# Two heads' masks first, then both heads' score products, in stick breaking and in FoX

## The reference, cut to what matters

```python
# stick breaking, 16 heads of width 64, scale 64**-0.5
z = jnp.einsum('bhtd,bhsd->bhts', qb, kb) * scale
strict = s_idx < t_idx
log_1m = jnp.where(strict, jax.nn.log_sigmoid(-z), 0.0)
suffix = lax.cumsum(log_1m, axis=3, reverse=True) - log_1m
a = jnp.where(strict, jnp.exp(jax.nn.log_sigmoid(z) + suffix), 0.0)
outs.append(jnp.einsum('bhts,bhsd->bhtd', a, vb))

# FoX, 8 heads of width 64, Fc = cumulative sum of the forget gates' logarithms
s = jnp.einsum('bhqd,bhkd->bhqk', qh, kh) * scale + Fc[..., :, None] - Fc[..., None, :]
p = jax.nn.softmax(jnp.where(mask, s, -jnp.inf), axis=-1)
outs.append(jnp.einsum('bhqk,bhkd->bhqd', p, vh))
```

## Time and profile before

| what | value |
|---|---|
| median of 3 runs | 1332.75 us (1332.71 to 1333.68) |
| the profiled execution's own time | 1331.95 us |
| its span, first to last instruction | 1330.2 us |
| DVE busy | 854.0 us (64%) |
| ACT busy | 708.3 us (53%) |
| DMA, mean rate | 168 GB/s |

### The profile page before, as it was taken

The page is one execution under the profiler, slowest core; times in us unless marked ns, Lnnn a source line. Parts: engine busy times, 40 slices in busy tenths (PEclk is TensorE's granted clock), DMA queues, the critical chain, the costliest instruction groups (busy, mean ns, idle before and its releaser), DMA issues.

```text
span 1330.2 us, 17683 instructions
## 1 busy us (share of the span) xinstructions
PE 1307.8 (98%) x7329; PEld 1124.8 (85%) x7329; DVE 854.0 (64%) x995; ACT 708.3 (53%) x968; POOL 110.7 (8%) x177
## 2 busy tenths in 40 slices
PE   7999999999999999999999999999999999999999
PEld 6888898988888988879888888898867888788887
DVE  4556755766666644367576666667875666787775
ACT  5655544544444676765454444565555764655553
POOL 7200100100000100020100000101330003000000
PEclk9999999999999999999999999999999999899999
DMA  8744643555555543244255555553434345455552
GB/s 257 254 159 142 210 149 118 183 190 188 191 189 207 167 158 127 96 159 159 95 190 191 190 190 191 181 197 96 159 127 158 129 156 176 140 190 190 190 191 95
DMA packets 156113, 223.64 MB, mean 168 GB/s; under 512 B 6103, under 2 KB 107635, under 8 KB 156032
## 3 DMA queue, kind: packets, MB, share of 16 engines
q1 hardware_dynamic: 154240, 218.18, 49.7%
q0 software_dynamic: 1664, 4.27, 1.0%
q10 hardware_dynamic: 128, 0.05, 0.0%
HBM read 221.44 MB, written 1.05 MB: 167 GB/s over the span
## 4 chain that ended last, share of the span: by engine, by line
PE 92%; DVE 4%; ACT 2%; POOL 1%; issue 1%; DMA 1%; SPq 0%; POOLq 0%; ACTq 0%
PE ps L397 18%; PE ps L399 9%; PE ps L421 9%; PE ps L423 9%; PE ps L422 9%; PE ps L382 5%; PE ps L383 5%; PE ps L384 5%; PE ps L559 4%; PE ps L560 4%; PE ps L561 4%; DVE wlo L1563 1%; PE ps L850 1%; PE ps L446 1%; ACT whi L1061 1%; PE ps L494 1%
## 5 line engine op out<-in xcount | busy, mean ns | idle before, releaser
L1061 ACT ACTIVATE whi<-raw 128x1024 fp32r<-128x1024 f32 x412 | 426.1, 1052 | 363.6 <-PE ps L397 167.4
L1563 DVE TENSOR_TENSOR wlo<-raw,whi 128x1024 fp32r<-128x1024 f32 x411 | 493.4, 1230 | 196.1 <-ACT whi L1061 192.8
L397 PE MATMUL ps<-RR,whi 128*128 128x512 f32 x1056 | 366.1, 397 | 0.8 <-DVE RR L1593 0.8
L399 PE MATMUL ps<-RR,wlo 128*128 128x256 f32 x1056 | 273.9, 280 | 0.1
L421 PE MATMUL ps<-whi,RR 128*128 128x512 f32 x592 | 237.5, 401 | 3.7 <-DVE ar L1626 1.6
L423 PE MATMUL ps<-whi,RR 128*128 128x512 f32 x592 | 231.0, 390 | 0.0
L422 PE MATMUL ps<-wlo,RR 128*128 128x512 f32 x592 | 230.9, 390 | 0.0
L397 PEld LDWEIGHTS ps<-RR,whi 128*128 128x128 f32 x1056 | 191.3, 188 | 37.8 <-DVE wlo L1563 1.2
L399 PEld LDWEIGHTS ps<-RR,wlo 128*128 128x128 f32 x1056 | 199.9, 189 | 12.3 <-DVE RR L1593 0.4
L382 PE MATMUL ps<-RR,whi 128*128 128x256 f32 x512 | 147.0, 287 | 1.7 <-DVE RR L1593 1.3
L383 PE MATMUL ps<-RR,whi 128*128 128x256 f32 x512 | 144.9, 283 | 0.0
(11 more groups left out here) (333 smaller groups left out, 1288.7 us busy)
## 6 DMA issues: line engine op xcount, KB each, us to landing
raw<-in_ffn_w_gate_up SPq DMA_DIRECT2D x44, 1024.0 KB, 5.1
raw<-in_ffn_w_down SPq DMA_DIRECT2D x33, 1024.0 KB, 4.9
raw<-in_w_in SPq DMA_DIRECT2D x28, 1024.0 KB, 5.0
raw<-in_ffn_w_up SPq DMA_DIRECT2D x22, 1024.0 KB, 5.1
raw<-in_xa_w_kv SPq DMA_DIRECT2D x16, 1024.0 KB, 5.2
raw<-in_sb_w_qkv SPq DMA_DIRECT2D x12, 1024.0 KB, 5.1
raw<-in_ml_w_in SPq DMA_DIRECT2D x11, 1024.0 KB, 5.7
raw<-in_xa_w_q SPq DMA_DIRECT2D x8, 1024.0 KB, 5.2
```

The source lines that it names most:

```text
L397: m = pe.matmul(two(ps[:, bank, :]), p.hi[:, k, :], XT2[:, k, :, :], start=k == 0, stop=k == 7)
L399: pe.matmul(ps[:, bank, 0:256], p.lo[:, k, :], X.h[:, k, :], start=False, stop=False)
L1061: act.activation(p.hi, p.raw, ACT.Copy).then_inc(S["w_hi"], 1)
L1563: dve.tensor_tensor(p.lo, p.raw, p.hi.bitcast(F32), ALU.subtract).then_inc(S["w_lo"], 2 if p.n == 2 else 1)
```

## The change

`sb_scores(p)` now issues the masks of both heads, then line 708's product of both heads, then line 709's product of both heads. `sb_z` is raised three times a pair (by the second head's first product and by both heads' last) and ACT waits for all three. `fox_head` becomes `fox_pair(g, j)`, with masks and selector products of both heads first and the f32 products of both heads behind them; `fx_s` is raised six times a group. PE's order around FoX is changed: `mqb` tile 1 now comes ahead of the wait for `fqT` and `fkT`; the pairs stand after `mqb` tile 1 and `gate0a` tile 1, and after `gate2a` tile 1 and `gate2b` tile 1. The wait for `yb_lo` moves behind `gate2a` tile 1.

```diff
             def sb_scores(p):
-                for h in range(2):
-                    o = ps[:, 4 + 2 * (p % 2) + h, :]
-                    r = slice(64 * h, 64 * h + 64)
+                both = [(ps[:, 4 + 2 * (p % 2) + h, :], slice(64 * h, 64 * h + 64)) for h in range(2)]
+                for o, r in both:
                     pe.matmul(o[:, 0:128], identb[:, :], mStr[:, :], start=True, stop=False, skip_group_check=True)
                     pe.matmul(o[:, 256:384], identb[:, :], mStr[:, :], start=False, stop=False, skip_group_check=True)
-                    pe.matmul(o[:, 0:256], kT[r, p, 0:128], qT[r, p, :], start=False, stop=False, skip_group_check=True)
+                for o, r in both:
+                    m = pe.matmul(o[:, 0:256], kT[r, p, 0:128], qT[r, p, :], start=False, stop=False, skip_group_check=True)
+                m.then_inc(S["sb_z"], 1)
+                for o, r in both:
                     m = pe.matmul(o[:, 256:384], kT[r, p, 128:256], qT[r, p, 128:256], start=False, stop=False,
                                   skip_group_check=True)
-                m.then_inc(S["sb_z"], 1)
+                    m.then_inc(S["sb_z"], 1)
...
-            def fox_head(g, h4):
...
+            def fox_pair(g, j):
+                n = 2 * g + j
+                both = [(ps[:, 4 + 2 * j + i, :], slice(64 * i, 64 * i + 64)) for i in range(2)]
+                for i, (o, r) in enumerate(both):
+                    sel = selr[:, 2 * n + i:2 * n + i + 1].to_broadcast([128, 128])
+                    pe.matmul(o[:, 0:128], identb[:, :], mRow[:, :], start=True, stop=False, skip_group_check=True)
+                    pe.matmul(o[:, 256:384], identb[:, :], mRow[:, :], start=False, stop=False, skip_group_check=True)
+                    pe.matmul(o[:, 0:128], sel, lg[:, 0:128], start=False, stop=False, skip_group_check=True)
+                    pe.matmul(o[:, 128:384], sel, lg, start=False, stop=False, skip_group_check=True)
+                for o, r in both:
+                    m = pe.matmul(o[:, 0:128], fqT[r, n, 0:128], fkT[r, n, 0:128], start=False, stop=False, skip_group_check=True)
+                m.then_inc(S["fx_s"], 1)
+                for o, r in both:
+                    m = pe.matmul(o[:, 128:384], fqT[r, n, 128:256], fkT[r, n, :], start=False, stop=True, skip_group_check=True)
                     m.then_inc(S["fx_s"], 1)
...
             tm_tile("mqb", X, 4, 8, 0, 0)
+            tm_tile("mqb", X, 4, 8, 1, 1)
...
-            fox_head(0, 0)
-            tm_tile("mqb", X, 4, 8, 1, 1)
-            fox_head(0, 1)
+            fox_pair(0, 0)
             pe.wait_ge(*at("fv_act", 1))
             tm_tile("gate0a", X, 0, 8, 2, 0)
-            fox_head(0, 2)
             pe.wait_ge(*at("f_cc", 1))
             tm_tile("gate0a", X, 0, 8, 3, 1)
-            fox_head(0, 3)
+            fox_pair(0, 1)
...
             tm_tile("gate2a", X, 0, 8, 2, 0)
-            pe.wait_ge(S["yb_lo"], 1)
-            fox_head(1, 0)
             pe.wait_ge(S["gate"], 2)
             tm_tile("gate2a", X, 0, 8, 3, 1)
-            fox_head(1, 1)
+            pe.wait_ge(S["yb_lo"], 1)
+            fox_pair(1, 0)
             tm_tile("gate2b", X, 4, 8, 2, 0)
-            fox_head(1, 2)
             tm_tile("gate2b", X, 4, 8, 3, 1)
-            fox_head(1, 3)
+            fox_pair(1, 1)
...
-                    act.wait_ge(S["sb_z"], i + 1)
+                    act.wait_ge(S["sb_z"], 3 * i + 3)
...
-                dve.wait_ge(S["fx_s"], g + 1)
+                dve.wait_ge(S["fx_s"], 6 * g + 6)
```

## The result

The changed kernel takes 1318.81 us (median of 4 runs, 1318.04 to 1319.46), the kernel before 1332.91 us in the same comparison (4 runs): a ratio of 0.9894, 95% interval 0.9881 to 0.9906. That is 14.1 us less; 1319.7 had been forecast. The two profiled executions took 1331.95 and 1319.46 us, 12.5 apart.

A forecast was written before the change was run, and what follows sets the result against it. PE was taken to bound the kernel; stick breaking's 7.1 and FoX's 5.9 us sum to 13.0, from 1331.95 to 1318.9, and with the median 0.8 above, 1319.7 us. Range 1317.5 to 1324.0.

The forecast's parts named there:

- What bounds the kernel: Whole kernel: PE, busy 98% of the span with 92% of the last chain, so shortening PE's order shortens the kernel.
- Side by side by row halves: Score parts: two heads on different row halves overlap wholly, so a pair costs one head's 0.85 us.
- first rival: Score parts: passes start strictly in issue order, overlap is partial, 2.6 us lost, 1322.3; chance 0.17 shared with loads in turn.
- Stick breaking: Eight pairs save 0.93 us each, 7.4 us, less 0.3 for a new wait: 7.1 us.
- new wait at the third pair: Stick breaking's third pair: PE waits 0.2 to 0.3 us for ACT's line 1344, and only there.
- FoX: Four pairs save 1.09 us each, 4.4 us, plus 1.5 for the covered wait: 5.9 us.
- covered wait: Ahead of FoX's first head: `mqb` tile 1 moved forward covers PE's idle of 1.52 us, saving 1.5 us.
- the entry: FoX: going from line 920's full-array product to the first f32 product costs 0.14 us, saved once a pair.
- the return: FoX: the projection behind the scores takes 0.10 us more to come back, saved once a pair.
- The sum: Whole kernel: stick breaking 7.1 plus FoX 5.9 saves 13.0 us.
- No case for slower: Slower rival, score parts: each change of row half stops PE, at 0.24 us making 1336.1 us; chance 0.03.
- The clock: PE's late stall: a fall from 2.4 to 1.2 GHz costs up to 2.4 us; 2 us either way.

The follow-up runs named there:

- products issued by head: Changed kernel with the first head's two products issued before the second head's two, in stick breaking and FoX: 1318.72 us, ratio to before 0.9888.
- the same half twice: Changed kernel with both heads of a pair reading rows 0 to 63, the first head's scores computed twice: 1325.77 us, ratio to before 0.9941.
- the changed kernel again: Changed kernel, unaltered, measured once more against the kernel before on another set's chip: 1319.04 us against 1332.37, ratio 0.9895.

## Why the prediction was right

*What bounds the kernel*: right. PE's order was shortened, and what it lost reached the end within the scatter of the stretches between and behind (0.4 us).

*Side by side by row halves*: right, taken over from the column halves of the earlier trace rows. The score part of a pair is 0.86 us against 0.85 forecast. The second half's passes start 0.007 to 0.014 us after the first half's. The products issued by head and the same half twice show that this is what it is. The first rival, passes strictly in the order of issue, is ruled out for row halves.

*Stick breaking*: 7.1 forecast, 7.43 measured. A pair saves 0.95 in place of 0.93, as the third and fourth masks follow 0.056 apart and not 0.07. The new wait at the third pair is there, 0.14 us and not 0.3. ACT's absolute value starts at 482.17, 0.11 ahead of the end of the copy before it (482.28), and not after it as I had reckoned; its wait of 0.50 us is gone, as forecast. With the 0.40 us taken off by which this trace's stick breaking starts later, that is 481.77 against the 481.93 reckoned: the 0.16 by which the new wait is shorter.

*FoX*: 5.9 forecast, 5.72 measured. The covered wait gave 1.68 and not 1.5, as the run with it alone shows. A pair gave the remaining 4.04 / 4 = 1.01 us and not 1.09. Two terms of that were mis-sized. One is the entry: I took line 920's product to need 0.12 us as one of line 382 does, but the next full-array product follows it after 0.17 (976.46 to 976.63). So to enter costs 0.26 - 0.17 = 0.09, as in stick breaking (0.08), and not 0.14. The other is the return: the first projection product behind a pair has 0.36 us to the second (977.99 to 978.35), and behind a single head 0.33, so a pair doesn't save the whole 0.10.

*The sum*: that 13.0 lies so near 13.15 is partly luck. Stick breaking came out 0.33 over its term, FoX's pairs 0.36 under theirs (4.04 against 4.4) and the covered wait 0.18 over.

*No case for slower*: the price of going from one half to the other is nothing that the traces show, 0.01 us instead of the 0.24 of that rival.

*The clock*: of either sign, as said, but the price was over-sized: 0.5 to 1.3 us, not up to 2.4. I had also cut its length at the end of my window: in the trace of before the half level goes on behind it, 0.77 on average from 1144 to 1148 us. And PE was not mostly idle in that window, as the forecast says, but busy for 4.73 of 7.80 us.

The clock explains a part of why the medians lie 14.1 apart and the stages 13.15. The medians of before were between 1332.37 and 1333.53 from one comparison to the next, those of the changed kernel 1318.81 and 1319.04. Seven of the 22 runs of before for which the clock is on record beside the experiments have a mean granted clock of 0.996, and they take 1333.53 to 1335.71 us; no run of the changed kernel is below 0.997. At 0.999, in the comparison of the changed kernel again, before takes 1331.76 and 1331.83 us and the changed kernel 1318.54 to 1319.09, 12.7 to 13.3 apart, as the stages say. So the gain is about 13 us. That the last 1 us of the 14.1 comes from such runs of the kernel before is likely and not shown: in that comparison its clocks are not on record, and none of the runs at 0.996 was traced. The changed kernel's four runs there fit the price of a fall, 1318.04 and 1318.18 us at 1.000 against 1319.44 and 1319.46 at 0.997, but its 1319.98 at 1.000, in the other comparison, does not.

## What to carry to other kernels

Where heads contract over 64 rows, look in the timeline for what stands between two heads' products: one full-array instruction keeps the halves apart and adds two changes of shape, some 0.2 us in all each way. Gather the full-array work of several heads (two and four were measured), then all the 64-row products. Their order among themselves didn't matter here. Since the halves run past each other, the kernels here raise the semaphore for the last product of each half; whether one raise would do was not tried. And when PE is the bound and waits for an engine, a tile that is due anyway and needs nothing from that engine belongs ahead of the wait; a bank shared for no reason can be what holds it back.

## What the runs showed of the hardware that was not expected

A change between the full array and 64 rows costs on both sides: 0.09 us to the first start, then 0.10 more for the first pass, and 0.09 with 0.10 on the way back (0.50 us of the first line 421 product, where the next has 0.40). In the first pass the weight load starts with the product itself, at 462.42 in the kernel before, while line 709's load starts at 462.74 and its product at 462.96:

```profile
462.42 0.30 PEld L708 LDWEIGHTS ps<-ar 64*128 64x128 f32 x2
462.74 0.40 PEld L709 LDWEIGHTS ps<-ar 64*128 64x128 f32 x2
```

Matmuls for different halves of the rows overtake each other. Issued by head, the second head's first pass starts 0.013 us behind the first head's first, ahead of three passes that were issued before it, and its weight load with it. Two bf16 products at full rate, one for each half, go in 0.06 us.
